# RWKV-7 in a decoder trunk on one core: the factors of key norm and group norm as powers taken by GpSimd

## The reference, cut to what matters

```python
def rwkv7_mixer(h, h_last, S0, mix, w_rkv, ...):
    ...
    kk = heads(k * k_k)
    kk = kk / jnp.maximum(jnp.sqrt(jnp.sum(kk * kk, axis=-1, keepdims=True)), 1e-12)
    r, k, v, decay, a = heads(r), heads(k), heads(v), heads(decay), heads(a)
    k = k * (1.0 + (a - 1.0) * k_a)
    o, S = _rwkv7_scan(r, decay, k, v, kk, a, S0)
    mu = jnp.mean(o, axis=-1, keepdims=True)
    var = jnp.mean(jnp.square(o - mu), axis=-1, keepdims=True)
    o = (o - mu) * lax.rsqrt(var + RW_GN_EPS)
    o = o * ln_w + ln_b
    o = o + jnp.sum(r * k * r_k, axis=-1, keepdims=True) * v
    return (o * g) @ w_o, S, h[:, -1]
```

## Time and profile before

| | |
|---|---|
| time, median of 3 runs | 3250.45 us (3242.67 to 3251.52) |
| the profiled execution: time | 3248.69 us |
| the profiled execution: span, first to last instruction | 3247.1 us |
| mean granted TensorE clock in it | 0.982 |
| TensorE (PE) busy | 3109.1 us, 96% |
| VectorE (DVE) busy | 1777.2 us, 55% |
| ScalarE (ACT) busy | 1100.3 us, 34% |
| GpSimd (POOL) busy | 131.0 us, 4% |

### The profile page before, as it was taken

How to read it: one execution, slowest core, us unless ns; L and a number is a source line. 1 busy time by engine, 2 the same in 40 slices (tenths; PEclk the granted TensorE clock), 3 DMA queues, 4 the chain that set the end, 5 groups by cost and what they waited for, 6 DMA issues and landing times.

```text
span 3247.1 us, 79829 instructions
## 1 busy us (share of the span) xinstructions
PE 3109.1 (96%) x34084; PEld 2948.7 (91%) x34084; DVE 1777.2 (55%) x2950; ACT 1100.3 (34%) x1825; POOL 131.0 (4%) x247
## 2 busy tenths in 40 slices
PE   8999999999999999997998887999999999899998
PEld 7998899999887999997987776999999988899998
DVE  6776643445676543445457886543445767643343
ACT  3222322223555321222345664322223323322222
POOL 0000000001322000000000000000000000000000
PEclk9999999999999999999998998999999999999999
DMA  3222222233433222232220000322222222222222
GB/s 128 99 88 71 86 84 91 85 99 98 137 124 108 85 88 87 87 99 68 70 66 15 21 24 12 91 91 91 85 92 83 86 86 93 67 89 94 79 97 72
DMA packets 104589, 268.94 MB, mean 83 GB/s; under 512 B 12802, under 2 KB 45954, under 8 KB 104146
## 3 DMA queue, kind: packets, MB, share of 16 engines
q1 hardware_dynamic: 91346, 228.54, 21.8%
q0 software_dynamic: 13056, 37.64, 3.5%
HBM read 247.61 MB, written 18.52 MB: 82 GB/s over the span
## 4 chain that ended last, share of the span: by engine, by line
PE 86%; DVE 7%; ACT 3%; DVEq 2%; issue 1%; DMA 0%; SPq 0%; ACTq 0%
PE ps L640 72%; PE ps L1105 3%; PE ps L1083 1%; PE ps L721 1%; DVE arena_r L2048 1%; DVEq L2646 1%; PE ps L938 1%; PE ps L1115 1%; PE ps L779 1%; PE ps L962 1%; PE ps L802 1%; DVE arena L2496 1%; DVE arena L2583 0%; PE ps L787 0%; DVE rstd L2017 0%
## 5 line engine op out<-in xcount | busy, mean ns | idle before, releaser
L640 PE MATMUL ps<-arena_r 128*128 128x272 f32 x11136 | 1499.5, 293 | 59.1 <-DVE arena_r L2502 19.2
L640 PEld LDWEIGHTS ps<-arena_r 128*128 128x128 f32 x11136 | 1431.4, 191 | 103.1 <-issue 53.8
L640 PE MATMUL ps<-hb_r,arena_r 128*128 128x272 f32 x8448 | 1064.0, 288 | 0.3 <-DVE hb_r L2041 0.3
L640 PEld LDWEIGHTS ps<-hb_r,arena_r 128*128 128x128 f32 x8448 | 1061.8, 188 | 1.1 <-DVE hb_r L2041 0.8
L1517 ACT ACTIVATE arena_r<-ring 128x1024 fp32r<-128x1024 f32 (+1 forms) x240 | 275.4, 1147 | 916.5 <-PE ps L640 916.5
L2067 DVE TENSOR_TENSOR arena_r<-ring,arena_r 128x1024 fp32r<-128x1024 f32 (+1 forms) x240 | 319.8, 1333 | 143.1 <-ACT arena_r L1517 143.1
L2113 DVE TENSOR_TENSOR arena<-ps,rstd 128x544 f32<-128x544 f32 x88 | 63.8, 724 | 294.1 <-PE ps L640 294.1
L2134 DVE TENSOR_TENSOR x<-x,ps 128x544 f32<-128x544 f32 x64 | 46.2, 722 | 294.1 <-PE ps L640 294.1
L1499 ACT ACTIVATE arena_r<-ring 128x1024 fp32r<-128x1024 f32 x80 | 84.6, 1058 | 134.4 <-PE ps L640 129.5
L1564 ACT ACTIVATE arena_r<-arena 128x544 f32 (+1 forms) x88 | 58.0, 659 | 196.4 <-DVE arena L2118 196.4
L1105 PEld LDWEIGHTS ps<-arena 64*64 64x64 f32 x4096 | 95.0, 140 | 30.9 <-ACT arena L1829 10.9
(11 more groups left out here) (403 smaller groups left out, 2784.6 us busy)
## 6 DMA issues: line engine op xcount, KB each, us to landing
ring<-in_w_up SPq DMA_DIRECT2D x176, 512.0 KB, 3.5
ring<-in_w_mix SPq DMA_DIRECT2D x112, 512.0 KB, 3.5
ring<-in_w_down SPq DMA_DIRECT2D x64, 704.0 KB, 4.1
arena<-in_hg_s POOLq DMA_DIRECT2D x16, 512.0 KB, 3.8
out_hg_so<-arena POOLq DMA_DIRECT2D x16, 512.0 KB, 2.9
ring<-in_w_hgout SPq DMA_DIRECT2D x16, 512.0 KB, 3.5
arena<-in_cache_k SPq DMA_DIRECT2D x128, 64.0 KB, 1.9
arena<-in_cache_v POOLq DMA_DIRECT2D x128, 64.0 KB, 2.3
```

Source lines behind the costliest of these rows:

```text
L640: mm = pe.matmul(PS[:, 2 * a + hf, 0:HALF], part[:, ws], rhs[:, o:o + HALF], start=start and n == 0, stop=stop and n == 2)
```

## The change

The root of the key norm on ScalarE, its reciprocal on VectorE, and both of the group norm are taken away. VectorE reads the key's sum of squares from PSUM with a maximum against 1e-24; ScalarE evicts the variance with scale and epsilon but with the function Identity. GpSimd then raises the tile, in place, to the power of minus one half: a `tensor_tensor` of the 128x544 tile with a column of -0.5 that is broadcast. It does so twice a pair, ahead of its wait for the state: `key_power(h + 1)`, then `norm_power(h - 1)`, and once ahead of the pairs and once behind them. VectorE waits for a new semaphore `rw_pow` in `rates` and in `normed`; the lists KEY_POW and NORM_POW count it. TensorE's `decay` waits for VectorE's maximum in place of ScalarE's root. The maximum moves to right behind level 2 on VectorE. ScalarE's root into the spare cell goes. Some waits and semaphores that another one covers go too.

```diff
+        c_table, c_half = cell[:, 62:63], cell[:, 63:64]
...
-        PREP_EV = ("kn_sq", "kn_rt", "w", "a", "exps")
+        PREP_EV = ("kn_sq", "w", "a", "exps")
+        KEY_POW = [1, 2] + [2 * n - 1 for n in range(2, HEADS)]
+        NORM_POW = [2 * g + 4 for g in range(HEADS - 2)] + [2 * HEADS - 1, 2 * HEADS]
...
# TensorE
                 def decay(n, a):
                     if n:
-                        pe.wait_ge(S("rw_prep_ev"), upto(PREP_EV, "kn_rt", n))
+                        pe.wait_ge(S("rw_kn_ev"), n + 1)
...
-                    pe.wait_ge(S("rw_hv_ev"), h + 1)
...
-                    pe.wait_ge(S("rw_u0_ev"), h + 1)
+                    pe.wait_ge(S("rw_post_ev"), 2 * h + 1)
...
-                    pe.wait_ge(S("rw_w_ev"), h + 1)
+                    pe.wait_ge(S("rw_post_ev"), 2 * h + 2)
...
-                            pe.wait_ge(S("rw_at"), h + 1)
                             pe.wait_ge(S("rw_rd"), h + 1)
...
# ScalarE
-                def key_root(n, a):
-                    act.wait_ge(S("rw_prep_mm"), upto(PREP_MM, "kn", n))
-                    act.activation(halves(rw_rn[n % 2]), acc(a), ACT.Sqrt).then_inc(S("rw_prep_ev"), 1)
...
                 def variance_root(g, a):
                     act.wait_ge(S("rw_gn_mm"), upto(GN_MM, "var", g))
-                    act.activation(halves(rw_sq), acc(a), ACT.Sqrt, scale=1.0 / HD, bias=c_gn).then_inc(S("rw_gn_ev"), 1)
+                    act.activation(halves(rw_sq), acc(a), ACT.Identity, scale=1.0 / HD, bias=c_gn).then_inc(S("rw_gn_ev"), 1)
...
-                    if former:
-                        act.activation(c_table, c_gn, ACT.Sqrt)
...
# VectorE
-                def key_norm(n, hf):
-
-                    rn = rw_rn[n % 2][:, hf * HALF:(hf + 1) * HALF]
-                    if hf == 0:
-                        dve.wait_ge(S("rw_prep_ev"), upto(PREP_EV, "kn_rt", n))
-                        dve.tensor_scalar(rw_rn[n % 2], rw_rn[n % 2], 1e-12, None, ALU.max)
-                        dve.drain()
-                    dve.reciprocal(rn, rn)
+                def key_norm(n, a):
+
+                    dve.wait_ge(S("rw_prep_mm"), upto(PREP_MM, "kn", n))
+                    dve.tensor_scalar(halves(rw_rn[n % 2]), acc(a), 1e-24, None, ALU.max).then_inc(S("rw_kn_ev"), 1)
...
                     dve.tensor_scalar(rw_k2[s], rw_be[s], -1.0, gain(V_KA, n), ALU.add, ALU.mult)
+                    dve.wait_ge(S("rw_pow"), KEY_POW[n])
                     dve.tensor_tensor(rw_kn[s], rw_kn[s], rw_rn[s], ALU.mult)
...
                 def normed(g):
                     o = of_pair(rw_R, g)
-                    dve.wait_ge(S("rw_gn_ev"), upto(GN_EV, "rt", g))
-                    dve.reciprocal(rw_sq, rw_sq)
-                    dve.drain()
+                    dve.wait_ge(S("rw_pow"), NORM_POW[g])
                     dve.scalar_tensor_tensor(o, o, gain(V_LNW, g), rw_sq, ALU.mult, ALU.mult)
...
                     level(h, 2)
+                    if more:
+                        key_norm(n, 0)
                     sample_first_level(h)
-                    if more:
-                        key_norm(n, 0)
                     level(h, 3)
                     if g >= 1:
                         gated(g - 1)
-                    if more:
-                        key_norm(n, 1)
                     sample_second_level(h)
...
# GpSimd
+                pool.memset(c_half, -0.5)
+                pool.drain()
+                pool.wait_ge(S("rw_kn_ev"), 1)
+                pool.tensor_tensor(rw_rn[0], rw_rn[0], c_half.to_broadcast([P, NT]), ALU.pow).then_inc(S("rw_pow"), 1)
                 pool.wait_ge(S("unit_done"), base + 3 * HEADS)
                 for h in range(2):
                     states(h)
+                def key_power(n):
+                    pool.wait_ge(S("rw_kn_ev"), n + 1)
+                    pool.tensor_tensor(rw_rn[n % 2], rw_rn[n % 2], c_half.to_broadcast([P, NT]), ALU.pow).then_inc(S("rw_pow"), 1)
+
+                def norm_power(g):
+                    pool.wait_ge(S("rw_gn_ev"), upto(GN_EV, "rt", g))
+                    pool.tensor_tensor(rw_sq, rw_sq, c_half.to_broadcast([P, NT]), ALU.pow).then_inc(S("rw_pow"), 1)
+
                 for h in range(HEADS):
                     if h + 2 < HEADS:
                         pool.wait_ge(S("rw_prep_mm"), upto(PREP_MM, "a", h))
                         hidden_weights(h + 2)
+                    if h + 1 < HEADS:
+                        key_power(h + 1)
+                    if h:
+                        norm_power(h - 1)
                     pool.wait_ge(S("rw_state"), h + 1)
...
+                norm_power(HEADS - 1)
                 pool.wait_ge(S("rw_sh_out"), 16)
```

More of the change, by code:

```diff
@@ L324, in build @@
         c_lam, c_sub, c_gn = cell[:, 14:18], cell[:, 18:19], cell[:, 19:20]
-        c_table = cell[:, 62:63]
+        c_table, c_half = cell[:, 62:63], cell[:, 63:64]
         ar = Arena(arena_t, ARENA)
@@ L1885, in pair @@
                     level(h, 1)
-                    if more:
-                        key_root(n, 0)
                     turned(h, 2)
@@ L1902, in pair @@
                     act.wait_ge(S("rw_y_mm"), INV * h + INV)
-                    act.activation(rw_hv[s], PS[:, 6, :], ACT.Copy).then_inc(S("rw_hv_ev"), 1)
+                    act.activation(rw_hv[s], PS[:, 6, :], ACT.Copy)
                     if former:
@@ L1909, in pair @@
                     act.wait_ge(S("rw_post_mm"), 2 * h + 1)
-                    act.activation(rw_nu, PS[:, 6, :], ACT.Copy).then_inc(S("rw_u0_ev"), 1)
+                    act.activation(rw_nu, PS[:, 6, :], ACT.Copy).then_inc(S("rw_post_ev"), 1)
                     act.wait_ge(S("rw_post_mm"), 2 * h + 2)
-                    act.activation(rw_w[s], PS[:, 7, :], ACT.Copy).then_inc(S("rw_w_ev"), 1)
-                    if former:
-                        act.activation(c_table, c_gn, ACT.Sqrt)
+                    act.activation(rw_w[s], PS[:, 7, :], ACT.Copy).then_inc(S("rw_post_ev"), 1)
                     state(0)
@@ L1962, in rwkv @@
                 unit(17)
-                key_root(0, 2)
                 unit(18)
@@ L2669, in pair @@
                     level(h, 2)
-                    sample_first_level(h)
                     if more:
                         key_norm(n, 0)
+                    sample_first_level(h)
                     level(h, 3)
@@ L2692, in pair @@
                     dve.drain()
-                    dve.tensor_tensor(in_order(rw_at[s]), in_order(rw_at[s]), two_banks(6, 0), ALU.add).then_inc(S("rw_at"), 1)
+                    dve.tensor_tensor(in_order(rw_at[s]), in_order(rw_at[s]), two_banks(6, 0), ALU.add)
                     r = in_order(of_pair(rw_R, h, 0, NP_TOK))
@@ L2774, in rwkv @@
                 rw_rest(layer, 18)
-                key_norm(0, 0)
-                key_norm(0, 1)
+                key_norm(0, 2)
                 rw_rest(layer, 19)
```

## The result

The changed kernel takes 4474.8 us (median of five runs, 4472.5 to 4475.1) where the kernel before takes 3250.2 (median of five, 3242.7 to 3251.5): a ratio of 1.378, with a 95% interval of 1.376 to 1.379. The forecast was 3273 us and its range ended at 3350. The direction was right, the size was off by a factor of fifty: +1225 us in place of +24.

What follows compares the result with a forecast made beforehand. TensorE was taken to bound the kernel, holding 86% of the chain that ended last. Terms 18.2 + 2.6 + 3.9 - 0.8 = +23.9 us on the profiled 3248.69 gave 3272.6, say 3273 us; range 3241 to 3350.

Steps and rivals of the forecast that it cites:

- D: Length of one GpSimd power on the 128x544 tile, twice a pair; taken as two VectorE reciprocals, 7.1 us.
- the upper bound of 10.6: Longest GpSimd power allowed for: logarithm, product and exponential at three VectorE reciprocals of 3.55 us, 10.6 us.
- the third rival: GpSimd's power is longer than three reciprocals; at four, 14.2 us, the kernel is 113 us slower, 3362 us; chance 15%.
- the signs of being wrong: D below 4 us, VectorE idling where no wait stands, or the key norm's power late at `rates`.
- The map behind D: Steps from D to time: six pairs 18.2 us, pair 7 2.6, after the last pair 3.9, set-up -0.8; sum +23.9.
- The break-even at 4.07 us: Group norm before VectorE's product: above D = 4.07 us, VectorE behind `normed` and TensorE are delayed by D - 4.07.
- The hand-off of 0.4 us: Around each GpSimd power: 0.3 us for GpSimd to wake plus 0.1 us back to VectorE.
- ScalarE's roots and loads at nothing: Removing eight roots and nine table loads (11.5 us) from ScalarE was priced at no gain.
- The new maximum of 0.72 us: VectorE's key norm maximum reading PSUM takes 0.72 us, eight times 6 us; its release of `decay` is covered by 0.5 us.
- The cover of the key's power up to 9.5 us: Key norm's power on GpSimd, wanted by VectorE at L2529, delays nothing up to D = 9.5 us.
- The gain of a short power: Rival case, D below 4.07 us: up to 7.7 us won in pairs; D = 0.7 gives -11 us, 3238; chance 28%.
- Rival 2: GpSimd's power blocks VectorE's instructions with two SBUF inputs in pairs 2 to 6: 23.5 us more, +47, 3296; chance 27%.

Runs made afterwards that it cites:

- the probe: The kernel before plus twelve single GpSimd instructions (multiplications, powers, a copy) on spare tiles behind layer 3's token mixer; a power of 128x544 took 87.11 us.
- five multiplications: The changed kernel with each of the 16 powers replaced by five GpSimd multiplications by a constant, factors left out: 3263.2 us, ratio 1.0054 to the kernel before.

## Why the prediction was wrong

**The step that failed is D**, "I take two reciprocals, 7.1 us", and with it the upper bound of 10.6. It measured 87.15 us. The bound was three of VectorE's reciprocals: the price of a step on one engine was carried to another engine that the trace had never shown computing. No row showed that a power is made of such steps there either, and the probe shows 158 ns for every column. Nothing in the trace of before excluded 87 us; the third rival said that GpSimd's arithmetic might be a program per element, and got 15% and four reciprocals where it was the case, some 25 reciprocals long (87.15 / 3.55). The range was made from a bound that wasn't one. That the kernel came out slower, as forecast, says only that D was above 4.07 us. Of the signs of being wrong that the prediction named, one came: the key's power was late at `rates`, by 77.5 us in pair 2.

**The map behind D held.** Put 87.15 in its own steps: six pairs by 87.15 - 4.07, pair 7 by 82.7, the tail by 84.0, less 0.8, make 664 us (the group norm's power alone measured +667). The key's power is late by 87.15 - 9.5 in seven pairs: 544. The prediction had no term for the set-up's own power, since 7.1 us were covered there; the set-up grew from 54.0 to 127.4 us, 73 more (with the key's alone 616, measured +601). Together 1281, less the 6 x 8.6 us that the two powers cover together: 1229, measured +1225. The 73 and the 8.6 were read from the changed kernel's own trace, so this sum is an account and no forecast; the independent marks are the kernels with one power, +601 and +667, and they too were forecast with the measured D.

**Point by point.** The break-even at 4.07 us is borne out by the sign that turns between 3.5 and 6.0, and by the 1.67 us in pair 3 (1.96 by the map). The hand-off of 0.4 us was 0.12. Behind the spread the map took the delay to pass on unchanged; with five multiplications pairs 1 to 5 grew by 3.1 us each, the rest being TensorE's lower clock. ScalarE's roots and loads at nothing: right within some 4 us. The new maximum of 0.72 us: right (0.71). The cover of the key's power up to 9.5 us: right to 1 us a pair. The gain of a short power was put at 11 us and is 15.5 for D = 1.1 and 19 for none; in the profiled executions some 4 us of the missing part lie in pair 0, with its clock, which no term of the sum had.

**Rival 2** took VectorE's instructions with two SBUF inputs to be held for the whole power. The trace shows 0.9 us. L2517 in the pair above has two such inputs, started 0.05 us after the second power and took 1.62 us in place of 0.72 (with the key's power alone, where no second power starts beside it, it takes 0.73); L2638, 0.4 us into the first, took 1.28 in place of 0.79; and later ones beside the same power kept their length:

```profile
2086.99 1.28 DVE L2638 SCALAR_TENSOR_TENSOR arena<-arena,vec 128x544 f32<-128x544 f32 x1
2088.34 0.72 DVE L2641 TENSOR_TENSOR arena<-arena 128x544 f32<-128x544 f32 x1
...
2092.89 0.72 DVE L2509 TENSOR_TENSOR h<-h 128x544 f32<-128x544 f32 x1
```

The Trainium skill, page "SBUF — State Buffer", section "Who interferes with whom", says that VectorE's instructions with two SBUF inputs contend with a GpSimd instruction that reads SBUF, and calls the shared ports an exclusive lock. By that L2641 and L2509 should have waited for the power's end at 2173.7. They didn't, so for this instruction the measurement decides. Beside short multiplications the two engines do get in each other's way. With five of them the key's stand-in in pair 3 ran from 1832.44 to 1840.71 us, 8.3 in place of the group norm's 6.0, and VectorE's instructions beside it were longer too:

```profile
1834.82 5.89 POOL L2933 TENSOR_TENSOR o<-o,cell 128x544 f32<-128x544 f32 x4 [1.27 <-issue]
```

```profile
1838.23 1.59 DVE L2507 TENSOR_TENSOR_SCAN o<-consts,o 128x544 f32<-128x544 f32 x1
1839.90 1.40 DVE L2509 TENSOR_TENSOR o<-o 128x544 f32<-128x544 f32 x1
```

L2509 takes 0.72 and the scan 1.28 where nothing competes. All of this stayed covered: `rates` wanted the factor at 1842.87.

## What to carry to other kernels

A function on an engine that the trace doesn't show computing has no upper bound in that trace: one instruction of it on a spare tile gives the price, and it should be had before the work is moved. When a step is moved to an idle engine, ask for the length at which it stops being covered (here 4.07 and 9.5 us): these numbers held to 1 or 2 us in the pairs that were looked at, for D from 1 to 87. And where a root and a reciprocal stand one behind the other, look for one function that is both on the engine that already has the first.

## What the runs showed of the hardware

- A power on GpSimd takes about 1 us + 158 ns a column, whatever the number of partitions (1, 16, 64 and 128 for 136 columns) and the exponent (-0.5 and 2.0); a multiplication of 128x544 takes 1.1 us. The Trainium skill, page "GPSIMD Engine Reference", section "Performance versus the Vector engine", has 1.96 times VectorE's time for an add, by which 1.4 us was estimated; the multiplication was quicker, and no run has an add.
- In the rows above, the power gets in VectorE's way for its first 0.9 us only.
- TensorE's granted clock was 0.58 to 0.60 in the changed kernel's pairs with two powers, and its 1100 matmuls took 40 to 42 us in place of 34.6 to 36.2. Most of that costs nothing, as GpSimd sets the pace. But behind the spread TensorE is in the loop: in pair 2 the sample state takes 1.97 us at a granted clock of 0.50, where it took 1.08 in pair 3 of before, and from its start to the next TensorE L1204 it is 3.6 us, before 1.9. In pair 0 a further fall of the clock came in one execution of the same code and not in another, for 3 us.
